# End of the mixing stage in another order, in a two-block transformer kernel on one core of Trainium2

## The reference

```python
y_a = dsa_mixer(...)    # sparse attention: keys chosen by top-k of an index score
y_b = gla_mixer(...)    # gated linear attention
y_c = conv_mixer(...)   # depthwise causal convolution, 31 taps, 256 channels
y_d = mla_mixer(...)    # latent attention
y = jnp.concatenate([y_a, y_b, y_c, y_d], axis=-1) @ w_out
x = x + y
```

```python
# dsa_mixer, per block of 128 queries; topk = min(256, L // 4) = 64
score = jnp.where(causal[None], score, -jnp.inf)
_, sel = lax.top_k(score, topk)
logits = einsum(q, k[sel]) * scale + bias        # 4 heads
p = jax.nn.softmax(logits, axis=-1)
return einsum(p, v[sel])

# conv_mixer
h = a * jax.nn.sigmoid(gate)
h = lax.conv_general_dilated(h, w_dw, ...) + b_dw   # 31 taps
return jax.nn.silu(rmsnorm_2(h, g_norm))

# mla_mixer, per block of 128 queries
logits = jnp.where(causal, einsum(q, k) * scale, -jnp.inf)   # 4 heads
return einsum(softmax(logits), v)
```

## Time and profile before

| | |
|---|---|
| median of 3 runs | 2925.38 us (2923.79 to 2929.37) |
| the profiled execution | 2922.53 us |
| its span, first to last instruction | 2920.7 us |
| PE busy | 2823.2 us, 97% |
| DVE busy | 1799.6 us, 62% |
| ACT busy | 1480.7 us, 51% |
| POOL busy | 784.4 us, 27% |
| chain that ended last | PE 91%, issue 3%, DVE 2%, ACT 2%, POOL 1% |
| HBM read | 541.80 MB, 186 GB/s over the span |

### The profile page before, as it was taken

One profiled execution on the slowest core, in us unless ns is written; L12 is line 12 of the kernel. 1 busy time (PEld: TensorE's weight loads), 2 busy tenths in 40 slices (PEclk: granted clock), 3 DMA queues, 4 the chain that ended last, 5 costly groups with the idle time before them and its releaser, 6 DMA issues.

```text
span 2920.7 us, 59510 instructions
## 1 busy us (share of the span) xinstructions
PE 2823.2 (97%) x23646; PEld 2698.8 (92%) x23646; DVE 1799.6 (62%) x2418; ACT 1480.7 (51%) x1974; POOL 784.4 (27%) x749
## 2 busy tenths in 40 slices
PE   6999999999999999999998999999889999997999
PEld 5999999999999999999976998999789999986999
DVE  4656747677558466476475555657856566487664
ACT  3434434445444344344455655647656466476663
POOL 1322402124314124043001321312713113065230
PEclk9999999999999999999998999999889999998999
DMA  8765666666656656667512554555225555541454
GB/s 302 255 248 194 234 243 198 213 207 230 238 201 232 217 203 229 221 223 238 200 44 65 187 193 133 186 193 168 80 96 186 196 165 185 179 155 43 166 187 151
DMA packets 151706, 546.35 MB, mean 187 GB/s; under 512 B 16688, under 2 KB 20576, under 8 KB 151136
## 3 DMA queue, kind: packets, MB, share of 16 engines
q1 hardware_dynamic: 147632, 534.84, 54.1%
q10 hardware_dynamic: 3888, 8.86, 0.8%
HBM read 541.80 MB, written 1.84 MB: 186 GB/s over the span
## 4 chain that ended last, share of the span: by engine, by line
PE 91%; issue 3%; DVE 2%; ACT 2%; POOL 1%; ACTq 1%; DMA 1%; SPq 0%; DVEq 0%; POOLq 0%
PE ps L419 28%; PE ps L420 27%; PE ps L421 27%; PE ps L446 2%; PE ps L712 1%; POOL sq L2223 1%; ACT sq L1148 1%; PE ps L812 1%; PE ps L796 1%; PE ps L785 1%; DMA modraw<-wmod 1%; DVE w_lo L399 0%; ACTq L1543 0%; PE ps L1060 0%; ACT h_hi L1183 0%
## 5 line engine op out<-in xcount | busy, mean ns | idle before, releaser
L399 DVE TENSOR_TENSOR w_lo<-raw,w_hi 128x1024 fp32r<-128x1024 f32 x874 | 1136.2, 1315 | 685.0 <-ACT w_hi L391 683.6
L419 PE MATMUL ps<-h_hi,w_hi 128*128 128x256 f32 x4928 | 1407.1, 286 | 17.1 <-DVE h_lo L1597 5.0
L420 PE MATMUL ps<-h_lo,w_hi 128*128 128x256 f32 x4928 | 1392.1, 282 | 0.0
L421 PE MATMUL ps<-h_hi,w_lo 128*128 128x256 f32 x4928 | 1390.5, 282 | 0.0
L391 ACT ACTIVATE w_hi<-raw 128x1024 fp32r<-128x1024 f32 x874 | 901.8, 1057 | 518.1 <-PE ps L421 516.9
L419 PEld LDWEIGHTS ps<-h_hi,w_hi 128*128 128x128 f32 x4928 | 931.7, 189 | 35.9 <-issue 18.7
L421 PEld LDWEIGHTS ps<-h_hi,w_lo 128*128 128x128 f32 x4928 | 949.9, 193 | 0.0
L420 PEld LDWEIGHTS ps<-h_lo,w_hi 128*128 128x128 f32 x4928 | 933.7, 189 | 1.1
L2257 POOL CAST u_hi<-ut 128x256 fp32r<-128x256 f32 (+1 forms) x258 | 232.4, 901 | 1500.5 <-DVE ut L1746 785.9
L419 PE MATMUL ps<-u_hi,w_hi 128*128 128x256 f32 (+1 forms) x2064 | 585.2, 284 | 0.0
L420 PE MATMUL ps<-u_lo,w_hi 128*128 128x256 f32 (+1 forms) x2064 | 583.4, 283 | 0.0
(11 more groups left out here) (313 smaller groups left out, 1816.9 us busy)
## 6 DMA issues: line engine op xcount, KB each, us to landing
raw<-wst SPq DMA_DIRECT2D x874, 512.0 KB, 3.4
modraw<-wmod SPq DMA_DIRECT2D x132, 512.0 KB, 5.2
headraw<-wmod SPq DMA_DIRECT2D x12, 512.0 KB, 9.9
mtab<-mixtabs ACTq DMA_DIRECT2D x2, 1673.5 KB, 7.2
xT<-xin ACTq DMA_DIRECT2D x2, 1024.0 KB, 23.4
atab<-attabs ACTq DMA_DIRECT2D x1, 1024.0 KB, 6.0
out<-xT SPq DMA_DIRECT2D x1, 1024.0 KB, 4.8
skew<-sqb ACTq DMA_DIRECT2D x1, 768.0 KB, 3.2
```

The costliest lines, as they stand in the source:

```text
L399: dve.tensor_tensor(w_lo[:, s, :], raw[:, s, :], w_hi[:, s, :], ALU.subtract).then_inc(S("lo_ready"), 1)
L419: pe.matmul(psum, wh, hi, start=start, stop=False)
L420: pe.matmul(psum, wh, lo, start=False, stop=False)
L421: return pe.matmul(psum, wl, hi, start=False, stop=stop)
```

## The change

Four things move; nothing is computed otherwise.

- Six taps fewer go with the units: units 14 to 19 have three instead of four. They come behind the loop.
- ScalarE, behind the root of the linear attention's norm: four taps, exponentials 0, two taps, copy of turn 0, exponentials 1, the last four taps, copy of turn 1, exponentials 2, then the convolution's square, copy of turn 2, the convolution's root, exponentials 3. Before, the last taps, the square and the root came ahead of exponentials 0.
- TensorE: turn 0 follows the sparse scores of step 2 directly, the sparse scores of step 3 come before `give_back` and values 0, and the sums for the convolution's norm come behind turn 2, in bank 5 instead of bank 7. The wait for the convolution's root stands before turn 3 instead of values 1.
- VectorE: `top(2)` comes ahead of the top-k rounds, four rounds ahead of the linear attention's product instead of two; scaling of values 0 stands between the sixth and the seventh of the eight rounds, scaling of values 1 behind `top(3)`, and both copies out come before the convolution's norm.

```diff
--- before.py
+++ after.py
@@ -51,7 +51,7 @@
 UQ, UKV = 18, 19
 N_UNITS = N_IN + 2
 KTAPS = 31
-TAPS = [0] * 9 + [4, 3, 2, 2, 3] + [4] * 6 + [3] * 4
+TAPS = [0] * 9 + [4, 3, 2, 2] + [3] * 11
 KEYS_AT = 11
 INDEX_AT = (4, 5, 6, 7, 8, 9, 10, 13)
 INDEX_BANK = (4, 5, 6, 4, 5, 6, 4, 5)
@@ -1080,23 +1080,24 @@
                 latent_scores(1)
                 need("d_n", 6, 6)
                 sparse_scores(2)
-                need("m_sqc", 1, 1)
-                for n in range(2):
-                    mm = pe.matmul(ps[:, 7, 0:T], ones, sqm[:, n, :], start=(n == 0), stop=(n == 1))
-                mm.then_inc(S("m_ssc"), 1)
                 turn(0)
+                sparse_scores(3)
                 need("b_oi", 2, 2)
                 give_back(5, 0, (0, 1), 2 * T).then_inc(S("b_ss"), 1)
                 values(0)
-                sparse_scores(3)
                 pe.wait_ge(S("gated"), hid + 2)
                 turn(1)
-                need("c_rt", 1, 1)
                 values(1)
                 turn(2)
+                need("m_sqc", 1, 1)
+                need("s_pt", 4, 2)
+                for n in range(2):
+                    mm = pe.matmul(ps[:, 5, 0:T], ones, sqm[:, n, :], start=(n == 0), stop=(n == 1))
+                mm.then_inc(S("m_ssc"), 1)
                 turn_back(0)
                 turn_back(1)
                 values(2)
+                need("c_rt", 1, 1)
                 turn(3)
                 values(3)
                 turn_back(2)
@@ -1502,11 +1503,7 @@
                 ins.then_inc(S("d_half"), 1)
                 need("b_ss", 2, 1)
                 act.activation(rm[:, 2 * T:3 * T], ps[:, 4, 0:T], ACT.Sqrt, bias=epsc[:, 0:1], scale=1 / 64).then_inc(S("b_rt"), 1)
-                taps(2 * KTAPS - made[0])
-                need("c_tap", 2 * KTAPS, 2 * KTAPS)
-                act.activation(sqm[:, 0:2, :], hc[:, :, :], ACT.Square).then_inc(S("m_sqc"), 1)
-                need("m_ssc", 1, 1)
-                act.activation(rm[:, 3 * T:4 * T], ps[:, 7, 0:T], ACT.Sqrt, bias=epsc[:, 0:1], scale=1 / 256).then_inc(S("c_rt"), 1)
+                taps(4)
 
                 def exponentials(k):
                     kc = P * (k % TT + 1)
@@ -1526,9 +1523,18 @@
                     ins.then_inc(S("s_pt"), 1)
 
                 exponentials(0)
-                for k in range(1, 4):
-                    turned(k - 1)
-                    exponentials(k)
+                taps(2)
+                turned(0)
+                exponentials(1)
+                taps(2 * KTAPS - made[0])
+                turned(1)
+                exponentials(2)
+                need("c_tap", 2 * KTAPS, 2 * KTAPS)
+                act.activation(sqm[:, 0:2, :], hc[:, :, :], ACT.Square).then_inc(S("m_sqc"), 1)
+                turned(2)
+                need("m_ssc", 1, 1)
+                act.activation(rm[:, 3 * T:4 * T], ps[:, 5, 0:T], ACT.Sqrt, bias=epsc[:, 0:1], scale=1 / 256).then_inc(S("c_rt"), 1)
+                exponentials(3)
                 need("c_n", 1, 1)
                 act.activation(hc[:, :, :], hc[:, :, :], ACT.Silu).then_inc(S("c_silu"), 1)
                 turned(3)
@@ -2121,7 +2127,8 @@
                 need("b_oi", 2, 1)
                 dve.reciprocal(rm[0:32, 2 * T:3 * T], rm[0:32, 2 * T:3 * T]).then_inc(S("b_oi"), 1)
                 top(1)
-                topk_rounds(1, range(0, 2))
+                top(2)
+                topk_rounds(1, range(0, 4))
                 need("b_ss", 2, 2)
                 then(dve.scalar_tensor_tensor(OB[:, :, :], OB[:, :, :], V("bo"),
                                               ps[:, 5, :].rearrange("p (a t) -> p a t", a=2), ALU.mult, ALU.mult))
@@ -2129,22 +2136,20 @@
                 for ch in range(2):
                     dve.wait_ge(S("ulo_ready"), hid + ch + 1)
                     dve.tensor_tensor(ut[:, ch, 0:T], OB[:, ch, :], Z[:, B_R + ch, :], ALU.mult).then_inc(S("gated"), 1)
-                top(2)
-                topk_rounds(1, range(2, 4))
+                topk_rounds(1, range(4, 6))
                 scale(0)
-                topk_rounds(1, range(4, 7))
-                scale(1)
-                topk_rounds(1, range(7, 8))
+                topk_rounds(1, range(6, 8))
                 topk_bias(1)
                 top(3)
+                scale(1)
+                values_out(0)
+                values_out(1)
                 need("c_rt", 1, 1)
                 then(dve.reciprocal(rm[:, 3 * T:4 * T], rm[:, 3 * T:4 * T]))
                 for ch in range(2):
                     ins = dve.scalar_tensor_tensor(hc[:, ch, :], hc[:, ch, :], V("cn", ch), rm[:, 3 * T:4 * T],
                                                    ALU.mult, ALU.mult)
                 ins.then_inc(S("c_n"), 1)
-                values_out(0)
-                values_out(1)
                 scale(2)
                 need("c_silu", 1, 1)
                 for ch in range(2):
```

## The result

The changed kernel takes **2906.6 us** in the median (5 runs, 2902.0 to 2915.4), the kernel before 2927.3 beside it (5 runs, 2923.8 to 2933.7). The ratio is 0.9935, 95% interval 0.9914 to 0.9957: faster by 21 us, of which the interval leaves 13 to 25. The prediction said 2907.4. Run once more, later, the unaltered changed kernel gave 2906.5.

The account below looks back on a forecast made before the run. Stage ends, where no engine is full, were taken to bound any gain: 8.5 + 10.4 + 2 x 1.6 us, less 1.0 for hand-overs and 3.4 for half clock, saves about 18, from 2925.38 to 2907.4; range 2899 to 2912.

Parts of the forecast that it names:

- Exponentials(0) 4.3 earlier: Second stage end, ScalarE: exponentials(0) done at 2664.4 instead of 2668.7, with drain, square, matmul and root moved behind exponentials(2).
- turn(1): Stage ends, TensorE: turn(1) may start at 2671.95 in the second stage, and at 2111.95 instead of 2119.54 in the first.
- The rounds decide turn(1): Second stage end: VectorE's four top-k rounds end at 2670.4, 0.65 us after give_back; TensorE waits 1.2 us before turn(1).
- Both loads on the path, 1.28 each, no drain: Stage ends, ScalarE: two added table loads of 1.28 us lie on the path, 2.56 us a stage, without a drain.
- Top(3) before its need: Second stage end, VectorE: top(3) ends at 2678.9, 1.3 us before exponentials(3) needs it.
- From turn(1) to the next stage: Both stage ends: 19.0 us from turn(1) to the next stage's first matmul, before any added half-clock cost.
- half clock for one of the two stages: After turn(1), TensorE's clock falls before values(1) in one of the two stages, costing 3.4 us there.
- Taps: Units 14 to 19: six taps leave each stage's loop, TensorE's wait for VB vanishes, 1.6 us per stage, bounds 0 and 2.6.
- half clock in both: Rival, stage ends: half clock in both stages and no gain in the units, saving 11, to 2914; chance 0.15.
- The drain: Rival, ScalarE's table switches: they cost their drain, 2.8 us more per stage, saving 12.4, to 2913; chance 0.05.
- No effect: Rival, stage ends: another copy, such as Silu behind c_n, fixes the end of the stage; 2925; chance 0.05.
- slower via GpSimd: Rival, stage ends: GpSimd's late additions hold up the square; at 4.6 us each the kernel comes to 2941 or 2938; chance 0.03.

## Why the prediction was right

The number was 0.8 us from the median. Its terms were less exact than that, and part of the closeness is luck: the saving was put at 18 and the medians give 21, while the kernel before, from whose 2925.4 the number was counted, came out at 2927.3 beside it. Inside the sum, too, errors cancelled.

- **Exponentials(0) 4.3 earlier**: right. They ended 13.3 us behind L985 (2660.79 in ScalarE's timeline), 13.3 forecast, 17.6 before.
- **turn(1)** was forecast 20.9 and 22.2 us behind L985 in the second and the first stage; it came at 21.9 and 20.7. The step that failed: each stage was taken to keep its own clock of before in the latent scores. That half clock fell into the other stage. The sum, 42.6 for 43.1, was right because the two errors, 1.0 and 1.5, have opposite signs.
- **The rounds decide turn(1)**: right. It waits 1.66 for VectorE (1.2 forecast).
- **Both loads on the path, 1.28 each, no drain**: right. The load's end to the operation is 0.02, and two more loads cost 3.0 and 2.8 us per stage. The Trainium skill ("ScalarE: Activation LUTs", What ACT_TABLE_LOAD costs) charges 2.66 us for each switch with its drain. By it that run would have shown an estimated 5.7 us per stage; the trace does not agree, with 0.02 between a load and its operation.
- **Top(3) before its need**: right, and by more than forecast. It ended at 2676.3, exponentials(3) could start at 2680.5; 1.3 had been given. ScalarE waits for it, 1.6 us, only with exponentials(3) ahead of the root and the gaps filled.
- **From turn(1) to the next stage**: forecast 19.0, measured 21.9 and 21.5. The step that failed is "half clock for one of the two stages": it fell in **both**. Its price per stage, put at 3.4, was 2.9 and 2.5 beyond the forecast 19.0, since values(1) cost 1.7 more and not 1.9, and turn(1) still ran at full clock in the first stage (1.11 us). Together 5.3 against the 3.4 in the sum. The 1.0 taken off for hand-overs and the 0.5 by which turn(1) came early covered most of the difference: the two stage ends were forecast to give 8.5 + 10.4 - 1.0 - 3.4 = 14.5 and gave 14.1. The 19.0 had kept the half clock of before in the last piece, values(3) (3.7 before and after), so what filling the gaps took off from turn(1) on, 4.3 and 4.6, is more than this price.
- **The tail**, last copy to L419: 6.77 us for the 6.78 forecast.
- **Taps**: 1.6 forecast, 2.0 and 2.1 measured, between the bounds 0 and 2.6. GpSimd's late additions ended by 2668.7, 5 us ahead of the square.
- **Sum**: 17.7 forecast, 18.2 in the stretches, 21 in the medians.

Of the rivals: "half clock in both" came true in its mechanism, but not at its price, as it had also left out the units' gain. The Trainium skill's sentence behind it ("TensorE: Matmul & The Clock Gate", PE-mode transpose) says that transposes don't count as busy in the same way. In these runs the clock fell in or behind turn(1) with its gaps and stayed at 1.00 with plain matmuls around it; whether transposes without gaps would hold it was not tried. The drain is excluded. "No effect" and "slower via GpSimd" did not come near.

## What to carry to other kernels

Where no engine is full, look for the piece that stands ahead of the chain and that nobody needs soon; moving it behind the first link paid here even at the price of two table loads. Don't add up the gains of two reorderings on one chain: either alone gave four fifths or more of what both gave in the two stage ends together. And where TensorE waits between short pieces, look at the granted clock of those pieces: filling the gaps with matmuls that do nothing gave 10 us at the two ends, where no filler stood in front of work that was ready. Read the clock again afterwards: in another order the same fillers ran at 0.56.

## What was not expected of the hardware

**Eight bytes of SBUF cost 25 us** in 2906 (above). The Trainium skill ("SBUF — State Buffer", Door 1: The DMA port swizzle) says that SBUF is read in lines of 16 bytes, and that each access that crosses to a new line pays. A shift by 8 could act in that way, but no run shows it; a shift by 16, which would tell it apart from other effects of the place, was not tried.

**The same matmuls run at another pace for a while at full clock.** The same feed-forward loop, 30 us of it in the kernel before and in the changed one, ahead of anything that the change touches:

```profile
1740.00:1770.00 30.00, 30.00 (x258) 30.00 (x257) 13.48 (x11) 10.81 (x11) 0.00 (x0) 1.00 0.58 190
```

```profile
1740.00:1770.00 30.00, 30.00 (x244) 30.00 (x243) 12.26 (x11) 10.62 (x10) 0.00 (x0) 1.00 0.53 175
```

258 matmuls against 244, with PE busy throughout and a clock of 1.00 in both. Counted in steps of 5 us in which at least half of the matmuls start over 0.1215 us apart, the profile of after has five such stretches behind its first 50 us, about 275 us in all, and that of before two, about 85. At 14 in 258, 190 us more of them would cost some 10 us (an estimate), and 11 is what the profiled spans' difference lacks against the 18.2 of the stretches. Most of it lies ahead of any changed code: the first mixing units began at 2008.3 for 2000.8 before. It may also be why single runs of one kernel spread over 13 us. The changed kernel run again had about as much of it, at the same places. The version with three idle matmuls had about 200 us of it and that with five 30: by the same estimate 9 of the 10.8 us by which its profiled execution was longer outside the stage ends. So medians of these kernels carry a few us that their code does not explain, and what starts such a stretch stays open.
